# Attention of subtracted maps: the first two blocks of scores side by side, then the first two groups of turned maps

## The reference

```python
def differential_attention(q, k, v, lam):
    scale = q.shape[-1] ** -0.5
    s = jnp.einsum('bqhmd,bkhmd->bhmqk', q, k).astype(jnp.float32) * scale
    p = jax.nn.softmax(s, axis=-1)
    a = (p[:, :, 0] - lam * p[:, :, 1]).astype(v.dtype)
    return jnp.einsum('bhqk,bkhe->bqhe', a, v)
```

## Time and profile before

| | |
|---|---|
| median of 3 runs | 3866.82 us (3862.12 to 3867.98) |
| profiled execution | 3870.88 us |
| its span, first to last instruction | 3869.1 us |
| mean granted TensorE clock | 0.944 |
| PE busy in the span | 3438.4 us (89%) |
| stage `attn_a`, first score to last product | 316.4 us |
| of that PE busy / DVE busy / ACT busy | 282.9 / 204.8 / 183.6 us |
| PE idle from there to the next stage's first matmul | 13.2 us |

### The profile page before, as it was taken

One profiled execution on the slowest core, in us unless ns is written; L12 is line 12 of the kernel. 1 busy time (PEld: TensorE's weight loads), 2 busy tenths in 40 slices (PEclk: granted clock), 3 DMA queues, 4 the chain that ended last, 5 costly groups with the idle time before them and its releaser, 6 DMA issues. The chain is left out here.

```text
span 3869.1 us, 51564 instructions
## 1 busy us (share of the span) xinstructions
PE 3438.4 (89%) x19840; PEld 2349.5 (61%) x19840; DVE 1162.4 (30%) x2735; ACT 921.1 (24%) x2084; POOL 491.0 (13%) x628
## 2 busy tenths in 40 slices
PE   6999989969998399999999689698799579999994
PEld 2444445545544377888778565565564368788873
DVE  1000167646622411101111143455672421011112
ACT  3100156634523011111111132343352211111111
POOL 0000124010000011111001230113300000000003
PEclk8999999989999699999999889899899789999997
DMA  6327355443032677877778630101303478998885
GB/s 209 109 97 116 102 172 175 142 115 120 1 118 96 228 249 250 275 246 260 252 250 275 196 127 1 47 4 45 82 1 108 144 265 310 322 318 305 314 318 208
DMA packets 379802, 674.34 MB, mean 174 GB/s; under 512 B 80144, under 2 KB 118208, under 8 KB 373376
## 3 DMA queue, kind: packets, MB, share of 16 engines
q1 hardware_dynamic: 343360, 543.69, 41.6%
q10 hardware_dynamic: 22864, 82.06, 5.8%
q0 software_dynamic: 13440, 46.80, 5.0%
HBM read 586.86 MB, written 91.83 MB: 175 GB/s over the span
## 5 line engine op out<-in xcount | busy, mean ns | idle before, releaser
L2133 PE MATMUL experts_gu_ps<-experts_xT,experts_wg 128*128 128x160 f32 (+1 forms) x4096 | 552.5, 288 | 4.5 <-DVE experts_xT L2062 2.5
L2133 PE MATMUL experts_gu_ps<-experts_xT,experts_wu 128*128 128x160 f32 (+1 forms) x4096 | 549.3, 287 | 0.0
L2133 PEld LDWEIGHTS experts_gu_ps<-experts_xT,experts_wg 128*128 128x128 f32 x4096 | 529.7, 192 | 19.3 <-issue 19.3
L2133 PEld LDWEIGHTS experts_gu_ps<-experts_xT,experts_wu 128*128 128x128 f32 x4096 | 524.8, 191 | 0.0
L2104 PE MATMUL experts_y_ps<-experts_wd,experts_hid 128*128 128x512 f32 x1024 | 452.3, 597 | 0.0
L515 PE MATMUL proj_pb_ps<-proj_ahead_w,proj_hT 128*128 128x512 f32 x960 | 415.6, 594 | 0.0
L2075 DVE TENSOR_TENSOR experts_hid<-experts_sil,experts_gu_ps 128x160 f32<-128x160 f32 (+1 forms) x256 | 78.0, 305 | 941.5 <-ACT experts_sil L2039 937.5
L2039 ACT ACTIVATE experts_sil<-experts_gu_ps 128x160 f32<-128x160 f32 (+1 forms) x256 | 74.5, 291 | 1106.6 <-PE experts_gu_ps L2133 1106.6
L2104 PEld LDWEIGHTS experts_y_ps<-experts_wd,experts_hid 128*128 128x128 f32 x1024 | 190.6, 190 | 231.3 <-issue 228.5
L515 PEld LDWEIGHTS proj_pb_ps<-proj_ahead_w,proj_hT 128*128 128x128 f32 x960 | 181.9, 191 | 223.7 <-issue 223.7
L2011 POOL DMA_INDIRECT moe<-experts_y,experts_ixs x32 | 51.2, 1601 | 1131.7 <-DVE experts_y L2079 1131.7
(11 more groups left out here) (381 smaller groups left out, 4270.5 us busy)
## 6 DMA issues: line engine op xcount, KB each, us to landing
experts_wg<-in_l_w_gate SPq DMA_DIRECT2D x64, 2048.0 KB, 8.4
experts_wu<-in_l_w_up SPq DMA_DIRECT2D x64, 2048.0 KB, 13.6
experts_wd<-in_l_w_down SPq DMA_DIRECT2D x64, 2048.0 KB, 11.4
attn_a_mod_w<-in_l_w_mod ACTq DMA_DIRECT2D x36, 1024.0 KB, 4.9
proj<-proj_ob ACTq DMA_DIRECT2D x60, 256.0 KB, 2.1
proj_ahead_w<-in_l_w_in SPq DMA_DIRECT2D x6, 2048.0 KB, 9.8
attn_near_bias<-lines SPq DMA_DIRECT2D x80, 128.0 KB, 2.8
mix_xr<-res SPq DMA_DIRECT2D x18, 512.0 KB, 3.8
```

The source lines that it names most:

```text
L2133: mm = nc.tensor.matmul(GU[f % 2][:, part, 0:N], w[:, h, k, c * P:(c + 1) * P], xT[:, k, :], start=(k == 0), stop=(k == KD - 1))
```

## The change

In the loop of PE's program, block 1 of the scores of item n + 3 moves from behind the first turned group of item n to ahead of it. Blocks 0 and 1 are then adjacent, and so are turned groups 0 and 1. The rest of the item's order, all other engines' programs, all waits and all buffers stay the same. Where the item ahead has only one block, or none, nothing changes. Where item n has only one turned group, the product with the values follows it directly.

```diff
                     ahead = n + AHEAD
                     todo = [j for j in range(len(chunks(ahead % NT)))] if ahead < ITEMS else []
                     turns = len(rounds(n % NT))
-                    if todo:
-                        score(ahead, 0)
+                    for j in todo[:2]:
+                        score(ahead, j)
                     turn_round(n, 0)
-                    if len(todo) > 1:
-                        score(ahead, 1)
                     if turns > 1:
                         turn_round(n, 1)
                     weigh_values(n, 0)
```

## The result

The changed kernel takes 3877.03 us (median of 10 runs, 3869.31 to 3881.47) against 3867.72 us for the kernel before (10 runs on the same chips, 3862.12 to 3872.61). The ratio is 1.0022, with a 95% interval of 1.0012 to 1.0032: slower by 0.2%, some 8 to 9 us. Later runs of the same kernel gave 1.0022 again (1.0013 to 1.0031).

A forecast was written before the change was run, and what follows sets the result against it. TensorE was taken to set the pace in the changed 316.4 us stage, with ACT's chain second. The items' terms summed to +7.5 us, less 1.6 for the clock +5.9, on 3866.8: 3872.7 us, range 3863 to 3879.

The forecast's parts named there:

- step 1: PE's switches between scores and turned maps: one return trip fewer, a gain of 0.36 us per item on paper.
- step 2: First product: ACT's copy of turned group 0 loses its cover; the product ends 0.16 us later, not 0.36 earlier.
- step 3: Long items' end: third product waits for ACT's chain of copies and exponentials; new period 8.32 us, from 7.94 in seven items.
- step 4: Short items (two transposes, then product): product starts 0.35 us later; counts in items 18 and 28, 0.7 us.
- Step 5: POOL's rotation starts 0.86 us later: items 9 to 11 cost +0.9 us, item 19 ends 1.0 earlier.
- Step 6: Item 20's fall of the granted clock is taken as gone, 1.6 us less: +7.5 becomes +5.9 us.
- drain rule: On TensorE, changing the tiling mode drains the engine; by it alone time would fall, 0.36 us per pair of switches.
- the prediction's last sign of being wrong: In the trace after: the prediction is wrong if granted clock moves by more than one item's worth.
- (c): ACT's copy is on time and only step 1 acts: 3860.9 us, 3859.3 without the clock fall; chance 0.07.
- (d): DVE sets the pace in more items than counted, so the change does nothing: 3866 to 3868 us; chance 0.08.
- (b): TensorE's longer pauses in long items bring clock falls, 1.4 to 1.6 us each; two give 3877.3 us; chance 0.18.
- (a): The clock fall at item 20 stays: 3874.3 us, on the very bound; chance 0.25.

The follow-up runs named there:

- the early rotation: Against the changed kernel, POOL may start the rotation for heads 2 and 3 after item 6 or 16; ratio to before 1.0008 (0.9999 to 1.0018).

## Why the prediction was right and where it was not

The forecast was 3872.7 us with the change just inside the bound of 0.2%; it came out just beyond, 4 us higher: inside the full range of 3863 to 3879, outside the forecast's own 3870 to 3875. The mechanism of steps 1 to 4 is shown, the sizes of steps 5 and 6 were off. The total is also closer than its parts, since a gain that I had not counted (items 24 and 25) hides 1.2 us of the misses. By groups of items, in the profiled stage:

| items | step | predicted | measured |
|---|---|---|---|
| 2, 3, 4, 7, 13, 14, 17, 22, 23, 27, 30, 31, 34 | 2, 3 | +5.4 | +5.9 |
| 18, 28 | 4 | +0.7 | +0.7 |
| 9 to 12 | 5 | +0.9 | +3.2 |
| 19 to 21 | 3, 5, 6 | -1.4 | +0.3 |
| 24, 25 | 4 | 0 | -1.2 |
| 32, 33 | 3, 4 | +0.3 | +0.7 |
| first scores to item 1 | 4 | 0 | 0.0 |
| sum | | +5.9 | +9.6 |

**Steps 1 to 4, right.** Group 0 at 1.92, ACT at 2.61, a period of 8.32 in items 3, 4, 10, 13, 14, 23, 30, 31 and 34, 7.66 in 7, 17 and 27, 5.07 in 18 and 28 (2.83 to the product; 5.08 expected from the sum). The kernels that touch ACT's chain agree within about 0.1 us with what the chain gives (8.32, 7.78 for 7.67, 8.10 and 7.88, 7.63). Reading item 15, which already had the new pattern, was worth more than adding up instructions. Two readings of the old periods were wrong: item 2 took 8.57 before, not 7.94 (its clock was 0.92), and items 3, 13 and 23 are shorter because two tiles are prepared in them instead of four. Item 2 came out 0.65 longer (clock 0.90), and item 22 too (8.58, but 8.32 with the early rotation, so 0.26 of it is POOL's); that is the 0.5 in the first row of the table. The Trainium skill's drain rule, cited in step 1 (TensorEngine Tiling (Array Packing), Key Properties), holds for the sign: 7.63 against 7.94 where nothing else stands in the way. That the gain comes from a drain, no run shows. As the whole of the forecast it would have failed.

**Step 5, mis-sized: the late start of POOL's rotation.** I had 0.86 us for items 9 to 11; they took 2.97 more, and item 12 another 0.25. PE and POOL in item 9 of after, and PE at the preparation in item 11 and in item 21:

```profile
...
568.92 3.77 PE L884 MATMUL attn_a_s_ps<-attn_a_ahead_kT,attn_a_ahead_qT 64*128 64x512 f32 x8
572.62 0.44 PE L896 MATMUL attn_a_t_ps<-ident,attn_a_a 128*128 128x128 f32 x2
...
```

```profile
...
573.22 1.90 POOL L595 TENSOR_TENSOR attn_a_ahead_t<-attn_a_ahead_q,attn_a_ahead_cos 128x512 f32<-128x512 f32 x1 [64.38 <-PE attn_a_t_ps L896]
...
```

```profile
...
592.70 0.79 PE L872 MATMUL attn_a_t_ps<-ident,attn_a_ahead_qr 128*128 128x128 f32 x4 [2.28 <-issue]
...
```

```profile
...
670.87 0.63 PE L872 MATMUL attn_a_t_ps<-ident,attn_a_ahead_qr 128*128 128x128 f32 x4 [1.26 <-issue]
...
```

Block 0 of item 9 in the kernel before:

```profile
...
566.82 1.84 PE L884 MATMUL attn_a_s_ps<-attn_a_ahead_kT,attn_a_ahead_qT 64*128 64x512 f32 x4
...
```

Item 9 begins at a low clock, behind the wait for DVE's bias. Before, block 0 took 1.84 us and group 0 followed at once. Now both blocks lie before group 0 and run slowly, 3.77 us (granted clock 0.74 over the item, 0.91 before), so the group starts 3.70 after the item instead of 1.77: 1.93 later, where I had 0.86. I took the full-clock price for an item whose start wasn't at full clock. The rotation itself was 0.4 us shorter than before (19.3 against 19.7), so the preparation in item 11 starts 1.55 us later, counted from the start of item 9. PE's wait at 592.70 is 2.28 us (it was 0.72), and behind it the clock had fallen again (0.87 over item 11, 1.00 before): the modulation product took 1.89 in place of 1.04, and what lies between the wait and it 1.57 in place of 1.00. That is the other 1.42 of the 2.97 us, a term that the prediction put at nothing; it is there in the second profile of the changed kernel too (item 11 takes 12.20). The two kernels that touch the rotation show the cause: old order in item 9 takes the wait to 1.27, an early start takes it away.

**Steps 5 and 6, items 19 to 21: a gain given back.** The factor did slip through before POOL, as expected, and the fall of the clock at item 20 did go: 8.31 at clock 1.00 in place of 9.08. But DVE then ran its subtraction into POOL's first instructions. The factor and the subtraction of item 19 after, then the subtraction before:

```profile
...
650.12 0.22 DVE L821 SCALAR_TENSOR_TENSOR attn_a_c<-attn_a_sums,attn_a_nlam,attn_a_r 128x1 f32<-128x1 f32 x1
...
650.87 2.62 DVE L830 SCALAR_TENSOR_TENSOR attn_a_a<-attn_a_e,attn_a_c 128x1280 f32<-128x1280 f32 x1
...
```

```profile
...
645.04 2.17 DVE L830 SCALAR_TENSOR_TENSOR attn_a_a<-attn_a_e,attn_a_c 128x1280 f32<-128x1280 f32 x1
...
```

The subtraction started 0.01 us after POOL's first instruction (650.86) and took 2.62 us, where it took 2.17 before, so item 19 gained 0.5 and not 1.0. And PE, early in items 19 and 20, then waited for POOL in item 21 (1.26 us at 670.87; the rotation took 19.9 us, before 18.6), which had no such wait before. The prediction treated item 21 as free. POOL's end was a second bound 2 us behind PE's (before, the rotation ended at 661.79 and PE's preparation began at 663.77), and whatever the two items before it gain is lost there.

**Step 6, the clock elsewhere.** After the bias wait of item 24 the clock didn't fall in item 25 (7.03 against 8.01 before): 1.0 us that I hadn't counted as a possible gain. In items 32 and 33 it fell in one profile of the changed kernel and not in the other. With item 20 (forecast) and item 11, the granted clock moved in three places or more, so the prediction's last sign of being wrong, a clock that moves by more than one item's worth, did come, though gains and losses nearly cancel. Each such event is worth 0.7 to 1.6 us, and they decide between 3 us more or less. What makes one happen and not the other stays open.

**The rivals.** (c), the copy in time after all, is refuted by item 14. (d), DVE hides everything, holds only for 8, 24 and 29. (b), more falls of the clock, has a part: one new fall in item 11, two fewer in 20 and 25. Its price with two falls, 3877.3 us, is the measured time almost exactly, but that is chance: its place, the long items, kept full clock (1.00 in items 3 and 14) and their extra time is ACT's chain. (a) did not happen.

## What to carry to other kernels

When work is moved ahead of an instruction, price the other engine's chain that starts there, down to the next place where the first engine waits for its end: here 0.86 us of delay became 0.4 to 0.8 us per item, against 0.36 saved. An order on one engine is only half a change; the same adjacency gained 0.3 us an item once ACT's order was changed with it. And a gain upstream of a resource that is nearly a bound (POOL's rotation) is given back at the next wait for it, so look for the smallest slack ahead before adding up gains.

## What the runs showed that I had not expected

The moment at which full clock comes back varies under one and the same order. Item 9 and the modulation product ahead of it come behind a wait of PE of 3.9 to 5.2 us in all 13 profiles, and block 0 runs slowly in all of them. Group 0 started 1.77 to 2.01 us after the item in the seven profiles with one block ahead of it, and 2.71 to 3.72 us in the six with two, where full clock gives 1.06 and 1.92. So the delay of group 0 is robust. But block 1, which in those seven comes right behind group 0, took 1.13 us in two of them (before is one), and 1.15, 1.39, 1.58, 1.61 and 1.95 us in the others. Over item 9 the granted clock was 0.68 to 0.91 with one block ahead (before has the highest), and 0.73 to 0.89 with two. So the lower clock of item 9 in the changed kernel (0.74 against 0.91) is not shown to come from the two blocks standing together. What sets the moment stays open.

DVE's subtraction of 128 x 1280 values took 1.55 us alone, 2.0 to 2.6 beside POOL's rotation and 3.3 to 3.8 beside POOL's work on the output of a finished head (L716, L717); a rotation took 18.6 to 19.9 us beside that work and 16.5 or 17.7 us when started early, where DVE had few such subtractions.
